# Rows of an expert block gathered and scattered in two transfers of 64 slots, the experts' start in another order, and the last stage's row norms ahead of its slot norms

## The reference, cut to what matters

```python
h2 = rms_norm(x, norm_ffn_gain)                      # 1088 rows of 1024 numbers
g_idx = top_k(softmax(h2 @ w_router_group + b), 1)   # 1 of 4 groups
e_idx = top_k(softmax(e_logits of that group), 2)    # 2 of its 8 experts
weights = g_p * e_p / sum(e_p)
for each expert e, in blocks of 128 slots:
    y = (silu(xblk @ w_gate[e]) * (xblk @ w_up[e])) @ w_down[e]   # 1024 -> 512 -> 1024
x = x + segment_sum(y * weight, by frame)
y_prompt, y_sample = rms_norm(x, norm_final_gain)
```

## Time and profile before

| | us |
|---|---|
| median of 3 runs | 1682.91 (1681.29 to 1684.02) |
| the profiled execution, its own time | 1686.34 |
| its span, first to last instruction | 1684.6 |
| mean granted TensorE clock | 0.983 |
| PE busy | 1607.2 |
| DVE busy | 1045.5 |
| ACT busy | 763.2 |
| POOL busy | 462.3 |

### The profile page before, as it was taken

The page is one execution under the profiler, slowest core; times in us unless marked ns, Lnnn a source line. Parts: engine busy times, 40 slices in busy tenths (PEclk is TensorE's granted clock), DMA queues, the critical chain, the costliest instruction groups (busy, mean ns, idle before and its releaser), DMA issues.

```text
span 1684.6 us, 23312 instructions
## 1 busy us (share of the span) xinstructions
PE 1607.2 (95%) x8417; PEld 1316.6 (78%) x8417; DVE 1045.5 (62%) x1259; ACT 763.2 (45%) x812; POOL 462.3 (27%) x452
## 2 busy tenths in 40 slices
PE   7999999999999999998999998899999999999993
PEld 6888777777878777887888887688888887777772
DVE  5311355555655425445555555788888888888885
ACT  4310342332333322213321213488788777777773
POOL 2310354352553404321001012322222222222224
PEclk9999999999999999999999999999999999999997
DMA  7222332332230413326533346599999999999976
GB/s 256 97 92 71 125 116 73 112 92 78 66 119 32 131 42 128 132 94 240 184 122 123 130 159 272 180 356 384 371 379 378 370 377 372 369 364 372 376 255 237
DMA packets 111573, 346.45 MB, mean 206 GB/s; under 512 B 16076, under 2 KB 44924, under 8 KB 85776
## 3 DMA queue, kind: packets, MB, share of 16 engines
q1 hardware_dynamic: 101072, 327.08, 52.4%
q0 software_dynamic: 10432, 18.45, 4.3%
HBM read 301.90 MB, written 65.34 MB: 218 GB/s over the span
## 4 chain that ended last, share of the span: by engine, by line
PE 34%; DMA 12%; DVE 3%; issue 2%; ACT 2%; SPq 0%; POOL 0%; POOLq 0%; ACTq 0%; DVEq 0%
DMA we_raw_odd<-in_w_experts 9%; PE banks_ffn L1843 5%; PE banks_ffn L1845 5%; PE banks_ffn L1844 5%; PE banks_ffn L1324 2%; PE banks_ffn L1326 2%; PE banks_ffn L1325 2%; PE banks_ffn L1311 2%; PE banks_ffn L1313 2%; PE banks_ffn L1312 2%; PE banks_ffn L1861 2%; PE banks_ffn L1863 2%; PE banks_ffn L1862 2%; DMA we_raw<-in_w_experts 1%; PE banks_ffn L1318 1%
## 5 line engine op out<-in xcount | busy, mean ns | idle before, releaser
L994 PE MATMUL p_bank<-w_hi,ht_hi 128*128 128x512 f32 x640 | 272.9, 426 | 3.7 <-POOL w_lo L922 2.1
L996 PE MATMUL p_bank<-w_hi,ht_lo 128*128 128x512 f32 x640 | 252.9, 395 | 0.0
L995 PE MATMUL p_bank<-w_lo,ht_hi 128*128 128x512 f32 x640 | 252.3, 394 | 0.0
L2018 DVE TENSOR_TENSOR we_lo_odd<-we_raw_odd,we_hi 128x2048 fp32r<-128x2048 f32 x96 | 216.0, 2288 | 13.2 <-ACT we_hi L1914 11.8
L2018 DVE TENSOR_TENSOR we_lo<-we_raw,we_hi 128x2048 fp32r<-128x2048 f32 x96 | 215.6, 2288 | 11.8 <-ACT we_hi L1914 10.1
L1843 PE MATMUL banks_ffn<-we_hi,x_hi 128*128 128x512 f32 x512 | 206.1, 403 | 9.5 <-DVE x_lo L2023 9.5
L1914 ACT ACTIVATE we_hi<-we_raw_odd 128x2048 fp32r<-128x2048 f32 x94 | 179.0, 1918 | 58.8 <-DMA we_raw_odd<-in_w_experts 40.8
L1845 PE MATMUL banks_ffn<-we_hi,x_lo 128*128 128x512 f32 x512 | 201.0, 392 | 0.0
L1914 ACT ACTIVATE we_hi<-we_raw 128x2048 fp32r<-128x2048 f32 x90 | 171.3, 1918 | 51.6 <-DMA we_raw<-in_w_experts 38.9
L954 POOL TENSOR_TENSOR beta<-beta,prod 128x512 f32<-128x512 f32 (+3 forms) x120 | 129.5, 1091 | 223.9 <-DVE prod L806 223.9
L806 DVE TENSOR_TENSOR_SCAN prod<-keep,prod 128x512 f32<-128x512 f32 (+3 forms) x120 | 126.8, 1085 | 86.5 <-ACT keep L643 77.9
(11 more groups left out here) (355 smaller groups left out, 3022.6 us busy)
## 6 DMA issues: line engine op xcount, KB each, us to landing
we_raw<-in_w_experts SPq DMA_DIRECT2D x96, 1024.0 KB, 20.0
we_raw_odd<-in_w_experts SPq DMA_DIRECT2D x96, 1024.0 KB, 20.5
w_raw<-in_w_main SPq DMA_DIRECT2D x80, 256.0 KB, 4.6
projected<-stage SPq DMA_DIRECT2D x80, 256.0 KB, 2.0
gates<-projected SPq DMA_DIRECT2D x9, 1024.0 KB, 4.9
qkvr<-projected SPq DMA_DIRECT2D x9, 768.0 KB, 4.2
o_nat<-mixed SPq DMA_DIRECT2D x9, 512.0 KB, 3.3
x_mid<-x_new SPq DMA_DIRECT2D x9, 512.0 KB, 2.9
```

The costliest lines, as they stand in the source:

```text
L994: pe.matmul(out, ht_hi[:, k, rows], w_hi[:, j], start=(k == 0), stop=False)
L995: pe.matmul(out, ht_hi[:, k, rows], w_lo[:, j], start=False, stop=False)
L996: last = pe.matmul(out, ht_lo[:, k, rows], w_hi[:, j], start=False, stop=(k == KD - 1))
L2018: dve.tensor_tensor(w_lo[odd][:, j], w_raw[odd][:, j], w_hi[:, slot].bitcast(F32), ALU.subtract).then_inc(split[slot], 1)
```

## The change

- An indirect gather of 128 slots becomes two of 64 slots (rows 0 to 63, rows 64 to 127), and so does the scatter that accumulates. The row numbers are kept as `half_frame` (64 partitions x 2 halves x blocks) beside `frame`; PE turns the table's halves apart, ACT copies them.
- Start of the experts: DVE does no low part until the slot table has been scattered; it does G0 and U0, then the rows' low part, then G1, U1; `late` moves from before to behind the first block's DVE work, and with it PE's turning of `later` and POOL's `late_scatter` (gather(2) now stands ahead of it). SP loads D0 and D1 of expert 1 only after the first two gathers have landed.
- Routing: `first_peak` has three links in place of four (numbers are compared as n/64, so that "is lower" can be added at once), the group mask one in place of two: 17 links in place of 21. The last two tiles are both chosen first, and then shared and assigned; `both`, `odds` and `pair` get a second copy for the last tile. ACT's last two high parts stand otherwise, and a Silu of one column is added at the end of merge.
- End: `move_y(end-3)` ahead of `hidden_high(end-2)` on ACT; DVE norms all rows ahead of both `norm_slots`; POOL takes the root of the second slots ahead of the first slots' store.

```diff
@@ count / tensor (merge)
-        pe.matmul(out[:, 0:EXPERTS], s.before_b[:], both[:], start=True, stop=True)
+        pe.matmul(out[:, 0:EXPERTS], s.before_b[:], both_of(t)[:], start=True, stop=True)
...
         count(pe, SAMPLE - 1)
-        keep_awake(pe, s, unread, 50)
+        keep_awake(pe, s, unread, 28)
         count(pe, SAMPLE, counts_of(SAMPLE))
-        keep_awake(pe, s, unread, 64)
+        keep_awake(pe, s, unread, 76)
@@ scalar (merge)
-        for j in range(2):
-            link.first_high(act, j)
+        link.first_high(act, 0)
         chance(act, SAMPLE - 1)
-        for j in range(2, 4):
+        for j in (1, 2):
             link.first_high(act, j)
         chance(act, SAMPLE)
+        link.first_high(act, 3)
+        act.activation(opened_early[:], s.ident[:, 0:1], ACT.Silu)
@@ first_peak
-        chain.link(dve.tensor_scalar(cand[:, 0:width], values, top, 64.0, ALU.is_lt, ALU.mult))
-        chain.link(dve.tensor_tensor(cand[:, 0:width], cand[:, 0:width], iota, ALU.add))
+        chain.link(dve.scalar_tensor_tensor(cand[:, 0:width], values, top, iota, ALU.is_lt, ALU.add))
@@ choose
-        chain.link(dve.tensor_scalar(group_hot[:], iota_g, peak[:, 1:2], None, ALU.is_equal))
-        chain.link(dve.tensor_scalar(group_hot[:], group_hot[:], -1.0, -MASKED, ALU.add, ALU.mult))
+        chain.link(dve.tensor_scalar(group_hot[:], iota_g, peak[:, 1:2], MASKED, ALU.not_equal, ALU.mult))
@@ vector (merge), last two tiles
-            if t < SAMPLE:
-                share(dve, t)
+        for t in (SAMPLE - 1, SAMPLE):
+            share(dve, t)
             assert assign(dve, t, t * PLACE_LINKS, counts_of(t)) == PLACE_LINKS
-            if t == SAMPLE:
-                share(dve, t)
@@ sync (experts)
-        for j in range(6):
+        for j in (G0, U0, G1, U1):
             load_piece(sp, j, 1, 1)
...
+        sp.wait_ge(first_gathered, 32)
+        sp.wait_ge(gathered, 32)
+        for j in (D0, D1):
+            load_piece(sp, j, 1, 1)
         load_gates(sp, 2, 0, 2)
@@ tensor (experts)
         for a in range(2):
+            slots = slice(a * (P // 2), (a + 1) * (P // 2))
+            pe.transpose(halves[:, a], table[:, slots, 0], s.ident[0:EXPERTS, 0:EXPERTS]).then_inc(table_turned, 1)
+        for a in range(2):
             pe.transpose(listed[:, a], table[:, :, a], s.ident[0:EXPERTS, 0:EXPERTS]).then_inc(table_turned, 1)
@@ scalar (experts)
-        act.wait_ge(table_turned, 2)
-        act.activation(frame[:, 0:EXPERTS], listed[:, 0], ACT.Copy).then_inc(frame_ready, 1)
+        act.wait_ge(table_turned, 4)
+        act.activation(half_frame[:, :, 0:EXPERTS], halves, ACT.Copy).then_inc(frame_ready, 1)
+        act.activation(frame[:, 0:EXPERTS], listed[:, 0], ACT.Copy).then_inc(share_ready, 1)
...
-        hidden_high(act, end - 2)
         move_y(act, end - 3)
+        hidden_high(act, end - 2)
@@ vector (experts)
-        for j in (G0, U0, G1, U1):
+        dve.wait_ge(link.scattered, 16 * 2 * TILES)
+        for j in (G0, U0):
             low_part(dve, j, 0, 0)
         rows_low(dve, 0)
-        link.late(dve)
-        block_dve(dve, 0, 0, before=False)
+        for j in (G1, U1):
+            low_part(dve, j, 0, 0)
+        block_dve(dve, 0, 0, before=False)
+        link.late(dve)
...
+        link.norm_rows(dve, 1)
         link.add_prev(dve)
-        for o in range(1, 5):
+        for o in range(2, 7):
             link.norm_rows(dve, o)
         link.add_shared(dve, turn_x)
-        link.norm_slots(dve, 0)
-        link.norm_rows(dve, 5)
         dve.wait_ge(d_used, end * 2 + 2)
         link.add_last(dve, y)
-        link.norm_rows(dve, 6)
-        link.norm_slots(dve, 1)
         for o in range(7, TILES):
             link.norm_rows(dve, o)
+        link.norm_slots(dve, 0)
+        link.norm_slots(dve, 1)
@@ gpsimd (experts)
         def gather_rows(pool, at, rows, done=gathered):
-            pool.indirect_dma_start(rows, None, io["h_mid"], bass.IndirectOffsetOnAxis(ap=at, axis=0),
-                                    bounds_check=last_frame, oob_is_err=False).then_inc(done, 16)
+            for a in range(2):
+                half = slice(a * (P // 2), (a + 1) * (P // 2))
+                pool.indirect_dma_start(rows[half], None, io["h_mid"], bass.IndirectOffsetOnAxis(ap=at[:, a], axis=0),
+                                        bounds_check=last_frame, oob_is_err=False).then_inc(done, 16)
...
-            pool.indirect_dma_start(io["x_mid"], bass.IndirectOffsetOnAxis(ap=scatter_at[:], axis=0), y_out, None,
-                                    bounds_check=last_frame, oob_is_err=False, compute_op=ALU.add).then_inc(y_scattered, 16)
+            for a in range(2):
+                half = slice(a * (P // 2), (a + 1) * (P // 2))
+                pool.indirect_dma_start(io["x_mid"], bass.IndirectOffsetOnAxis(ap=scatter_at[:, a:a + 1], axis=0),
+                                        y_out[half], None, bounds_check=last_frame, oob_is_err=False,
+                                        compute_op=ALU.add).then_inc(y_scattered, 16)
...
+        set_scatter(pool, 0, first=True)
+        set_gather(pool, 2)
+        gather(pool, 2)
         link.late_scatter(pool)
@@ gpsimd (final)
+        root(pool, SQUARES["slots1"], TILES + 1)
         pool.wait_ge(slots_normed, 1)
         store_slots(0, io["y_sample"][0], at_sample, last_sample)
-        root(pool, SQUARES["slots1"], TILES + 1)
```

More of the change, by code:

```diff
@@ L1205, in merge @@
     hot_rows = sb("hot_rows", [P, 2 * TILES, EXPERTS])
-    both = sb("both", [P, EXPERTS], BF16)
+    both, both_last = sb("both", [P, EXPERTS], BF16), sb("both_last", [P, EXPERTS], BF16)
     place, picked = sb("place", [P, EXPERTS]), sb("picked", [P, 2, EXPERTS])
@@ L1339, in route, with both_of @@
         last.then_inc(routed, 1)
+    def both_of(t):
+        return both_last if isinstance(t, int) and t == SAMPLE else both
     def counts_of(t):
@@ L1346, in count @@
         pe.wait_ge(hot_done, t + 1)
-        pe.matmul(out[:, 0:EXPERTS], s.before_b[:], both[:], start=True, stop=True)
-        pe.matmul(out[:, EXPERTS:], s.ones_b[:], both[:], start=True, stop=True).then_inc(counted, 1)
+        pe.matmul(out[:, 0:EXPERTS], s.before_b[:], both_of(t)[:], start=True, stop=True)
+        pe.matmul(out[:, EXPERTS:], s.ones_b[:], both_of(t)[:], start=True, stop=True).then_inc(counted, 1)
     def step_pe(pe, t, branches=True, o_next=True, output=True, routes=True, first=False, second=False):
@@ L1424, in h_evac, with odds_of @@
         act.activation(h_turned[:], turn[:], ACT.Copy).then_inc(h_out, 1)
+    def odds_of(t):
+        return (odds_last, pair_last) if isinstance(t, int) and t == SAMPLE else (odds, pair)
     def chance(act, t):
         act.wait_ge(hot_done, t + 1)
+        odds, pair = odds_of(t)
         rel = s.group_rel[:, bass.ds(t, 1)].rearrange("p a g -> p (a g)")
@@ L1521, in choose @@
         chain.link(dve.tensor_scalar(hots, hots, s.valid[:, bass.ds(t, 1)], None, ALU.mult))
-        dve.tensor_tensor(both[:], hot_rows[:, bass.ds(t * 2, 1)].rearrange("p a e -> p (a e)"),
+        dve.tensor_tensor(both_of(t)[:], hot_rows[:, bass.ds(t * 2, 1)].rearrange("p a e -> p (a e)"),
                           hot_rows[:, bass.ds(t * 2 + 1, 1)].rearrange("p a e -> p (a e)"), ALU.add).then_inc(hot_done, 1)
@@ L1536, in assign @@
         chain.mark(dve.tensor_scalar(slot_f[:, 0], at, float(P), float(NOWHERE), ALU.is_ge, ALU.mult))
-        chain.link(dve.scalar_tensor_tensor(slot_f[:, 1], s.number[:, bass.ds(t * 2, 2)], float(P), at, ALU.mult,
+        chain.link(dve.scalar_tensor_tensor(slot_f[:, 1], s.number[:, bass.ds(t * 2, 2)], 64.0 * P, at, ALU.mult,
                                             ALU.add))
@@ L1758, in experts @@
     listed_later = banks[:, 7, 2 * EXPERTS:2 * EXPERTS + 2 * LATER].rearrange("p (a e) -> p a e", a=2)
+    halves = banks[0:P // 2, 7, P:P + 2 * EXPERTS].rearrange("p (a e) -> p a e", a=2)
+    halves_later = banks[0:P // 2, 7, 2 * P:2 * P + 2 * LATER].rearrange("p (a e) -> p a e", a=2)
     table_in, table_turned, frame_ready, share_ready = (
@@ L1819, in sync @@
         sp.sem_inc(rows_begun, 1)
-        sp.wait_ge(y_scattered, end * 16 - 32)
+        sp.wait_ge(y_scattered, end * 32 - 64)
         sp.sem_inc(rows_begun, 1)
@@ L1825, in turn_rows @@
         if first:
-            pe.wait_ge(first_gathered, 16)
+            pe.wait_ge(first_gathered, 32)
         else:
-            pe.wait_ge(gathered, i * 16)
+            pe.wait_ge(gathered, i * 32)
             pe.wait_ge(x_low, i)
@@ L1885, in tensor @@
         gate_up(pe, 1, 1)
+        down(pe, 0, 0)
+        turn_hidden(pe, 1)
         pe.wait_ge(later_in, 16)
         for a in range(2):
+            slots = slice(a * (P // 2), (a + 1) * (P // 2))
+            pe.transpose(halves_later[:, a], later[:, slots, 0], s.ident[0:LATER, 0:LATER]).then_inc(later_turned, 1)
             pe.transpose(listed_later[:, a], later[:, :, a], s.ident[0:LATER, 0:LATER]).then_inc(later_turned, 1)
```

(18 more changed lines are left out.)

30 lines of the change are left out of this document (18 added, 12 removed).

## The result

The changed kernel took 1690.19 us (median of 11 runs, 1686.66 to 1693.65), the kernel before 1684.46 (11 runs, 1681.29 to 1687.06): ratio 1.0035, 95% interval 1.0025 to 1.0046. It is slower by a third of a per cent, where 1664 was forecast, and outside the range. Its profiled execution spans 1689.9 us, 5.3 more than that of before. Executions over 1.5% above the fastest of their kernel (one of e13's four, one of the kernel before's) are left out of every ratio in this text, but not of the medians.

A forecast was written before the change was run, and what follows sets the result against it. PE bounds the experts at 17.72 us a block, later DMA at 18.6 through eight loaded engines. From 1686.34 profiled, -13.8 - 3.4 + 2.0 - 4.0 = -19.2 gives 1667.1, as median of runs 1664, range 1659 to 1669.

The forecast's parts named there:

- part 1: Experts' loop: two transfers of 64 balance the engines, so PE's pace holds throughout; -13.8 us, range 0 to -14.5.
- PE's pace of 17.72: Experts' loop: PE's own time for a block in us, taken as the pace throughout after the change.
- the eight loaded engines: Experts' later blocks: filled slots 0 to 63 lie on eight engines, which need 19.1 us a block while others wait.
- the lead that is used up by block 17: Experts' loop: DMA, slower than PE all along, uses up a lead of some 13 us, then bounds the loop.
- The mean of 0.266 a row: Queue q0: engine time in us for each 4 KB row, gathered and scattered rows taken together.
- the block by block sum: Experts' loop after the split: at 0.243 us a row, the worst engine falls behind by at most 9 us.
- POOL's loop: Experts: four indirect DMAs a block for two cost POOL 0.6 to 4.5 us more, taken as 2, hidden by idle time.
- Part 2: Routing and start of the experts: first matmul 3.4 us earlier, DVE's later work costing +2.0.
- DVE's pile-up: Start of the experts: work moved behind the first matmul delays PE's block 2 by +2.0 us, bounds 0 and +4.
- Part 3: End: row norms ahead of slot norms -3.3 us, `y_out` ahead of ACT's high part -0.7; -4.0 in all.
- The first, that halves don't balance: Experts' loop: pace stays 18.6 us a block, only start and end change; 1676 us, chance 0.12.
- The third: Experts: POOL's loop of scatter, gather and landings becomes the bound, 19.1 us a block; 1702 us, chance 0.04.

The follow-up runs named there:

- e13: The changed kernel with each 1 MB weight piece also loaded in two transfers of 64 neighbouring partitions: 1991 us.
- e2: The changed kernel with the gather whole again (128 rows) and only the scatter in two transfers of 64: faster than either kernel, last 28 periods 17.7 us.
- e7: The changed kernel with the halves of gather and scatter taken as every second partition instead of 0-63 and 64-127: 1690.87 us.
- e9: e5 with the changed end of the last stage (all row norms ahead of both slot norms): 1665.45 us.
- e5: The kernel before, whole transfers of 128 rows, with slots reordered over the partitions so every engine gets 4 to 6 rows: 1666.88 us.
- e14: e12 with the two transfers of each weight piece on every second partition instead of on 0-63 and 64-127: 1683.61 us.
- e12: The kernel before with each weight piece in two transfers of 64 neighbouring partitions, gather and scatter whole: 223 GB/s from 1400 to 1600 us.

## Why the prediction was wrong

**The failed step** is in part 1: "Slots 0 to 63 now put four slots on each engine: 14.8 + 4 x 2 x 0.266 = 16.9 us." It moves the row count from eight to four and keeps the price of rows and weights. It took it that a transfer into 64 neighbouring partitions moves each packet as fast as one into 128. It doesn't: a gathered row took 0.239 instead of 0.159, and the share of weight packets that take 0.34 to 0.70 us rose from 3% to 15%. With the packets of the changed kernel, an engine with six rows needs, by estimate, 48 x 0.332 (85% at 0.309, 15% at 0.465, the mean of the slow ones) + 6 x 0.239 + 6 x 0.327 = 19.4, one with eight 20.5; measured are 19.4 mostly. From the turn of block 3 to the last, before took 508.9 us and after 515.2: **+6.3 where -13.8 was predicted.** In e2 it is 496.5: -12.4, where some -12.6 of the predicted -13.8 fall ahead of the last turn. So the balance was worth what the prediction said, once the gather is left whole.

**The rest of what bounds the kernel** stands: PE's pace of 17.72, weights of 14.8, the eight loaded engines, the lead that is used up by block 17. The mean of 0.266 a row hid that an added row costs 0.327 and a gathered one 0.159 (mean 0.243, the very figure the block by block sum used).

**POOL's loop** had time to spare in after; with the gaps between them four issues take 8.5 us a block in place of 4.2. That is 4.3 more, twice the 2 taken, but within 0.6 to 4.5 and hidden. (The lower bound of 0.6 is 3.9 + 0.9 - 4.2; the prediction's bracket has 0.6 where the three gaps of 0.9 belong.)

**Part 2**: first matmul -3.4 predicted, -2.9 from the landmark. Behind it DVE's pile-up was sized at +2.0 against an upper bound of 4; it is 4.9, 2.0 net by block 3 (-1.4 was predicted). The chain above shows it: `late` until 1087.5, five low parts until 1100.3, then hidden. DVE's line itself was nearly right: `x_lo` of block 2 was forecast 37.6 us after the first matmul and ended 38.5 after it. What the sum left out is the clock behind PE's wait, 1.6 us at 0.51; where the other 1.3 lie was not followed. In the profiles part 2 comes to +1.0, since after's stage before was done 0.95 earlier.

**Part 3**: -4.0 predicted, measured from the last turn to the end -2.0 (65.3 for 67.3), about -0.5 where the loop isn't bound by DMA, and nothing in e7 (67.7). The parts sum to 6.3 + 1.0 - 2.0 = 5.3, the difference of the spans.

**The rivals.** None had the mechanism. The first, that halves don't balance, gave 1676. The third had the right sign with the wrong place. The rule that speaks against the change, that 64 neighbouring partitions take half the rate, is in the Trainium skill, "SBUF — State Buffer", Door 1; the prediction draws on the same page for another matter and gives this rule no chance. One was due.

**The best version** is e9 (1665.45) or e5 (1666.88), which the runs can't tell apart: before's whole transfers with the slots dealt evenly over the engines.

## What to carry to other kernels

Before splitting a transfer to balance engines, ask which partitions each piece covers: keep every piece over the whole partition range (whole, or every second partition), and move the elements instead, so that the filled ones lie on all engines. Judge transfers by GB/s at a full share and by the length of single packets, not by the share. And price a saving at the start of a stage where the loop reaches its steady pace, with the clock behind any new gap on PE, not at its first matmul.

## What was unexpected of the hardware

- An 8 KB packet into SBUF takes 0.309 us (median) in whole or alternating transfers (before, e14), and 0.57 when each transfer covers 64 neighbouring partitions (e12); a 4 KB gathered row takes 0.159 against 0.31 in the same two kernels.
- The slowing reaches packets of other queues: in e12 whole gathers slow to 0.31 us beside halved weights, and in after weight packets with a gathered row in flight take 0.43 in the median, the others 0.313. In before both medians are 0.309.
- A 4 KB row added in memory takes 0.327 us, twice a gathered one, whether in transfers of 64 or 128 (e2, before).
- A skipped slot still has a packet, of 4 or 8 bytes and 9 ns: before shows some 57 of 8 bytes a block, for 60 empty slots in the mean.
- Twelve weight transfers a block instead of six cost nothing (e14, 1.0000 [0.9987, 1.0013]).
